# Chunk ends ahead of outputs in the S5 scan, and a bias table turned by TensorE

## What is computed

```python
def s5_mixer(u, ...):                     # 64 groups of 16 channels, 64 complex states each
    bu = einsum(u, bb)                    # inputs of the states
    s = associative_scan(a, bu)           # s[t] = a * s[t-1] + bu[t], over 512 steps
    y = einsum(s.re, c_re) - einsum(s.im, c_im) + d_skip * u
    y = gelu(y)
    return y * sigmoid(y @ w_glu + b_glu)
s5_branch = (s5_mixer(u) * silu(z)) @ w_out          # u, z = split(h @ w_in)

def sliding_window_attention(q, k, v, sinks, rel_bias):   # 16 heads, windows of 128
    s = q @ k.T * HEAD_DIM ** -0.5
    dist = qi + WINDOW - kj               # bias depends on the distance alone
    s = where(valid, s + rel_bias[t5_bucket(dist)], -1e30)
    p = softmax([s, sink]);  o = p @ v
```

## Time and profile before

| | |
|---|---|
| median of 3 runs | 3879.19 us (3876.99 to 3879.67) |
| the profiled execution: its own time | 3886.67 us |
| its span, first to last instruction | 3884.5 us |
| mean granted clock of TensorE | 0.951 of full |
| busy: TensorE, weight load | 92%, 71% |
| busy: VectorE, ScalarE, GpSimd | 58%, 28%, 37% |
| chain that ended last: TensorE, VectorE, issue, GpSimd | 71%, 15%, 7%, 3% |
| S5 scan, first flip to last y | 2565.5 to 2771.5 us |
| GLU product, output product | 2771.5 to 2839.3, 2839.3 to 2892.8 us |

### The profile page before, as it was taken

How to read it: one execution, slowest core, us unless ns; L and a number is a source line. 1 busy time by engine, 2 the same in 40 slices (tenths; PEclk the granted TensorE clock), 3 DMA queues, 4 the chain that set the end, 5 groups by cost and what they waited for, 6 DMA issues and landing times.

```text
span 3884.5 us, 44649 instructions
## 1 busy us (share of the span) xinstructions
PE 3576.9 (92%) x15779; PEld 2775.4 (71%) x15779; DVE 2239.8 (58%) x3073; ACT 1104.7 (28%) x1787; POOL 1424.2 (37%) x696
## 2 busy tenths in 40 slices
PE   6999999899998999999989999878879888999898
PEld 5888766678886888776678887667656565766676
DVE  5443487764434443378685433678564568476763
ACT  1222233322223222233332222311223442333332
POOL 3444553344443444453344444320122113311342
PEclk9999999999999999999899999986689889999999
DMA  3333321223333332332133323331262112211221
GB/s 100 95 88 96 96 71 41 68 86 94 89 95 88 94 95 88 99 88 54 28 93 96 96 87 104 75 91 48 73 114 60 33 38 64 57 36 44 78 87 55
DMA packets 622119, 299.40 MB, mean 77 GB/s; under 512 B 96925, under 2 KB 616590, under 8 KB 621982
## 3 DMA queue, kind: packets, MB, share of 16 engines
q1 hardware_dynamic: 618494, 287.50, 26.7%
q0 software_dynamic: 2592, 7.87, 1.2%
q10 hardware_dynamic: 896, 2.23, 0.2%
HBM read 287.58 MB, written 9.96 MB: 77 GB/s over the span
## 4 chain that ended last, share of the span: by engine, by line
PE 71%; DVE 15%; issue 7%; POOL 3%; ACT 3%; DMA 1%; DVEq 0%; SPq 0%; ACTq 0%; POOLq 0%
PE ps L319 21%; PE ps L328 21%; PE ps L320 21%; POOL WL L257 2%; PE ps L1002 2%; PE ps L2235 2%; POOL YP L1590 1%; PE ps L2233 1%; DMA RAW<-a_w_out 1%; DVE Y L1557 1%; PE ps L970 1%; DVE SS L421 1%; PE ps L991 1%; PE ps L489 1%; PE ps L1074 1%
## 5 line engine op out<-in xcount | busy, mean ns | idle before, releaser
L257 POOL TENSOR_TENSOR WL<-RAW,WH 128x1024 fp32r<-128x1024 f32 (+4 forms) x606 | 1314.7, 2171 | 2331.6 <-ACT WH L279 2331.4
L319 PE MATMUL ps<-UH,WH 128*128 128x512 f32 x3056 | 1246.7, 408 | 100.9 <-DVE UL L737 39.2
L320 PE MATMUL ps<-UL,WH 128*128 128x512 f32 x3056 | 1217.2, 398 | 0.0
L279 ACT ACTIVATE WH<-RAW 128x1024 fp32r<-128x1024 f32 (+4 forms) x605 | 570.9, 944 | 1333.1 <-PE ps L328 1288.1
L328 PE MATMUL ps<-UH,WL 128*128 128x512 f32 x3056 | 779.9, 397 | 11.0 <-POOL WL L257 11.0
L319 PEld LDWEIGHTS ps<-UH,WH 128*128 128x128 f32 x3056 | 589.5, 193 | 271.8 <-issue 56.7
L320 PEld LDWEIGHTS ps<-UL,WH 128*128 128x128 f32 x3056 | 589.3, 193 | 130.1 <-issue 7.6
L328 PEld LDWEIGHTS ps<-UH,WL 128*128 128x128 f32 x3056 | 576.4, 190 | 145.4 <-POOL WL L257 13.5
L1463 DVE TENSOR_TENSOR T<-ps,R 128x512 f32<-128x512 f32 x88 | 60.9, 691 | 392.7 <-PE ps L328 392.7
L319 PE MATMUL ps<-HH,WH 128*128 128x512 f32 x704 | 279.2, 397 | 0.0
L320 PE MATMUL ps<-HL,WH 128*128 128x512 f32 x704 | 276.9, 393 | 0.0
(11 more groups left out here) (432 smaller groups left out, 3972.0 us busy)
## 6 DMA issues: line engine op xcount, KB each, us to landing
RAW<-w_ff_in SPq DMA_DIRECT2D x176, 512.0 KB, 3.8
RAW<-w_in SPq DMA_DIRECT2D x72, 512.0 KB, 3.9
RAW<-w_ff_out SPq DMA_DIRECT2D x64, 384.0 KB, 3.2
RAW<-w_ff_out SPq DMA_DIRECT2D x64, 320.0 KB, 3.1
RAW<-d_w_in SPq DMA_DIRECT2D x24, 512.0 KB, 3.8
RAW<-b_w_in SPq DMA_DIRECT2D x17, 512.0 KB, 3.8
RAW<-w_out SPq DMA_DIRECT2D x16, 512.0 KB, 3.7
RAW<-w_ple_gate SPq DMA_DIRECT2D x16, 512.0 KB, 3.7
```

Of the source, the lines that this page charges most:

```text
L257: e.tensor_tensor(m.WL[:, s, 0:k, :], m.RAW[:, r, 0:k, :], m.WH[:, s, 0:k, :].bitcast(F32), ALU.subtract).then_inc(m.low_ready.sem, 1)
L279: e.activation(m.WH[:, s, 0:k, :], m.RAW[:, r, 0:k, :], ACT.Copy).then_inc(m.high_ready.sem, 1)
L319: e.matmul(out, m.WH[:, s, c, 0:t.cols], H[:, k0 + c, :], start=(x == 0 and c == 0), stop=False)
L320: e.matmul(out, m.WH[:, s, c, 0:t.cols], L[:, k0 + c, :], start=False, stop=False)
```

## The change

It has two parts.

1. In Chunks.tensor the block of ends(k) stands ahead of the block of y(k-1), with all its waits. Nothing else of S5 is touched.
2. The bias table. BROW goes to DRAM once (skew, 16 x 384, 24 KB) from SP's queue. SP reads BIAS from it with a partition step of one element, so that partition q has the shift P-1-q: the table upside down. A new step Turnover multiplies it by a reversed identity (FLIP, a new constant, loaded with the others) in eight matmuls of 128x512 (two heads each) and copies each product back into BIAS on ScalarE. Turnover runs inside Renorm, behind the root. The loads go out at unit 2, the one-hot matmul and its VectorE steps behind tile 2, the write at unit 6, the read at unit 7; GpSimd's two DMAs and the step Unskew go. BiasReady and the value flip wait for the copies.

```diff
@@ -702,6 +702,8 @@
         m.next_root = None
+        self.beside = m.beside_root
+        m.beside_root = None
         self.x0 = m.x_new.reserve(DC)
@@ -714,10 +716,14 @@
         self.root.tensor(e)
+        if self.beside is not None:
+            self.beside.tensor(e)
...
         self.root.scalar(e)
+        if self.beside is not None:
+            self.beside.scalar(e)
         if self.next_gain is None:
@@ -2221,6 +2228,18 @@
                             yield
+                        if k < DC:
+                            e.wait_ge(inputs_ready.sem, k + 1)
+                            e.wait_ge(u2_in[k], 16 * TC)
+                            if k > 0:
+                                e.wait_ge(states_ready.sem, k)
+                            for n in range(2):
+                                for t in range(4):
+                                    for g in range(2):
+                                        ins = e.matmul(m.ps[half(g), 7, (4 * n + t) * NC:(4 * n + t + 1) * NC], L1[:, n, t, half(g)],
+                                                       U2[:, 4 * k + t, g, :], start=True, stop=True)
+                            ins.then_inc(ends_made.sem, 1)
+                            yield
                         if k >= 1:
@@ -2235,18 +2254,6 @@
                             ins.then_inc(y_made.sem, 1)
-                            yield
-                        if k < DC:
-                            e.wait_ge(inputs_ready.sem, k + 1)
-                            e.wait_ge(u2_in[k], 16 * TC)
-                            if k > 0:
-                                e.wait_ge(states_ready.sem, k)
-                            for n in range(2):
-                                for t in range(4):
-                                    for g in range(2):
-                                        ins = e.matmul(m.ps[half(g), 7, (4 * n + t) * NC:(4 * n + t + 1) * NC], L1[:, n, t, half(g)],
-                                                       U2[:, 4 * k + t, g, :], start=True, stop=True)
-                            ins.then_inc(ends_made.sem, 1)
                             yield
@@ -2420,21 +2427,22 @@
                         cu.go("sync", e)
+                    if j == 2:
+                        rel_load.issue(e)
                     if j == 6:
-                        rel_load.issue(e)
+                        e.wait_ge(m.flip_free.sem, rel.b + 1)
+                        e.dma_start(skew, BROW[:]).then_inc(skewed, 16)
+                    if j == 7:
+                        e.wait_ge(skewed, 16)
+                        e.dma_start(BIAS[:], bass.AP(skew.tensor, 0, [[1, P], [3 * P, SWA_HEADS], [1, 2 * P]])).then_inc(skewed, 16)
                 def tensor_tail(self, e, i, n):
-                    if n == 6:
+                    if n == 2:
                         rel.tensor(e)
...
                 def vector_tail(self, e, i, n):
-                    if n == 6:
+                    if n == 2:
                         rel.vector(e)
-
-                def gpsimd_tail(self, e, i, j):
-                    if j == 7:
-                        e.wait_ge(m.flip_free.sem, rel.b + 1)
-                        e.dma_start(skew.rearrange("h q x -> h q x"), BROW[:].unsqueeze(1).to_broadcast([SWA_HEADS, P, 3 * P])).then_inc(skewed, 16)
             add(RestOfChunks(cu))
@@ -2455,27 +2463,40 @@
                 return f
-            rel_load = Load([(RELB[0:32, :], a["rel_bias_2"], swa_in), (RELB[32:33, :], a["c_masked"], swa_in), (HOT[:], a["c_hot"], swa_in),
+            rel_load = Load([(RELB[0:32, :], a["rel_bias_2"], swa_in), (RELB[32:33, :], a["c_masked"], swa_in), (HOT[:], a["c_hot"], swa_in), (FLIP[:], a["c_flip"], swa_in),
                              (SINK[:], a["b_sinks_2"][0].partition_broadcast(P), swa_in)])
...
             def rel_pe(e, bank):
-                e.wait_ge(swa_in, 64)
+                e.wait_ge(swa_in, 80)
                 return e.matmul(bank[0:SWA_HEADS, 0:3 * P], RELB[:], HOT[:], start=True, stop=True)
...
                 e.wait_ge(*v.last)
-                e.wait_ge(swa_in, 64)
+                e.wait_ge(swa_in, 80)
                 e.tensor_scalar(SINK[:], SINK[:], 8.0, None, ALU.mult).then_inc(*v.next())
-            class Unskew(Step):
-                def gpsimd(self, e):
-                    e.wait_ge(skewed, 16)
-                    src = bass.AP(skew.tensor, P - 1, [[3 * P - 1, P], [P * 3 * P, SWA_HEADS], [1, 2 * P]])
-                    e.dma_start(BIAS[:], src).then_inc(skewed, 16)
+            class Turnover(Step):
+
+                b0, o0 = bias_turned.reserve(SWA_HEADS // 2), bias_out.reserve(SWA_HEADS // 2)
+                flips = m.flips.total
+
+                def tensor(self, e):
+                    e.wait_ge(skewed, 32)
+                    e.wait_ge(m.flip_free.sem, self.flips)
+                    for g in range(SWA_HEADS // 2):
+                        if g > 1:
+                            e.wait_ge(bias_out.sem, self.o0 + g - 1)
+                        e.matmul(m.ps[:, 4 + g % 2, :], FLIP[:], BIAS[:, 2 * g:2 * g + 2, :], start=True, stop=True).then_inc(bias_turned.sem, 1)
+
+                def scalar(self, e):
+                    for g in range(SWA_HEADS // 2):
+                        e.wait_ge(bias_turned.sem, self.b0 + g + 1)
+                        e.activation(BIAS[:, 2 * g:2 * g + 2, :], m.ps[:, 4 + g % 2, :].rearrange("p (h x) -> p h x", h=2),
+                                     ACT.Copy).then_inc(bias_out.sem, 1)
             wg = chunks(a["a_w_glu_2"][0])
@@ -2483,7 +2504,7 @@
             out_gemm(chunks(a["a_w_out_2"][0]), UF, (M2H, M2L), gg.s0)
-            add(Unskew())
+            m.beside_root = Turnover()
@@ -2512,7 +2533,8 @@
                 return ins
-            fl = Flips(m, [(turn_values, lambda g, e, bank: e.tensor_copy(VB[:], bank.rearrange("p (t x) -> p t x", x=P)).then_inc(*g.frees()))])
+            fl = Flips(m, [(turn_values, lambda g, e, bank: e.tensor_copy(VB[:], bank.rearrange("p (t x) -> p t x", x=P)).then_inc(*g.frees()))],
+                       needs=[(bias_out.sem, bias_out.total)])
             fl.t0 = m.tiles + 1
@@ -2530,7 +2552,7 @@
                 def vector(self, e):
-                    e.wait_ge(skewed, 32)
+                    e.wait_ge(bias_out.sem, bias_out.total)
             add(BiasReady())
@@ -2908,7 +2930,8 @@
         k_dram = nc.dram_tensor("k_dram", [DC, P, P], F32, kind="Internal").ap()
-        skew = nc.dram_tensor("skew", [SWA_HEADS, P, 3 * P], F32, kind="Internal").ap()
+        skew = nc.dram_tensor("skew", [SWA_HEADS, 3 * P], F32, kind="Internal").ap()
+        bias_turned, bias_out = [Signal(ctx.enter_context(nc.semaphore(n))) for n in ("bias_turned", "bias_out")]
...
```

More of the change, by code:

```diff
@@ L1319, in build @@
             BIAS = sb("BIAS", [P, SWA_HEADS, 2 * P], F32, ph)
+            FLIP = sb("FLIP", [P, P], F32, ph)
         with ExitStack() as ph:
@@ L1450, in build @@
                   needs=[(const_in, 16 * 4)], splits=DC, squares=DC))
-        m.next_root = None
+        m.next_root = m.beside_root = None
         def ffn(l, w_in, w_out, next_gain):
@@ L2976, in constants @@
             "c_tri": (np.arange(P)[:, None] <= np.arange(P)[None, :]).astype(np.float32), "c_selg": selg,
-            "c_ident": np.eye(P, dtype=np.float32),
+            "c_ident": np.eye(P, dtype=np.float32), "c_flip": np.eye(P, dtype=np.float32)[::-1].copy(),
             "c_mask": np.where(np.arange(P)[None] > np.arange(P)[:, None], np.float32(MASKED), np.float32(0))}
```

## The result

The changed kernel takes 3897.48 us (median of 7 runs, 3894.09 to 3904.32), the one before 3879.67 in the same comparison (7 runs): ratio 1.0042, interval 1.0032 to 1.0052, so 16.3 us slower (12.4 to 20.2). The forecast was 3891 with a range of 3878 to 3901. The profiled execution of the changed kernel took 3898.65 us, its span is 3896.7 and its granted clock 0.950. Against the profiled execution of before (3886.67, span 3884.5) this is +12.2 in the span.

A forecast was written before the change was run, and what follows sets the result against it. TensorE, busy 92% of the span, was taken as the bound. S5 +20 and bias table -8.0 made +12 on the profiled 3886.67 us, 3898.7; less the profile's 7.5 above the median, 3891, range 3878 to 3901.

The forecast's parts named there:

- The loop behind the GEMM: S5 groups 4 to 7: y starts 13.0 us after the CA_ fill in three intervals, +6.0 us in sum.
- The last step gains nothing: S5, y(7): still waits for MT loads behind y(6)'s stores, 9.3 us from store to y(7); no gain.
- Rival B: S5's last step: y(7) starts on its states, some 2.5 us sooner, moved ends hidden; total 3869; chance 0.05.
- The woven intervals: S5 groups 0 to 3, inside the GEMM: y slips behind moved tile halves, ends and copies; +14 us taken.
- Rival A: S5 tiles 4 to 7: moved halves are absorbed, part 1 costs 6 to 8, total 3877 to 3879; chance 0.16.
- the difference carries over: Whole kernel: the profiled execution's 7.5 us above the median holds after the change too, so 3898.7 becomes 3891.
- VectorE beside GpSimd: Last GLU tiles: L2453 gives back 4.1 us spent beside the write, L2455 takes 2.2 more in two tiles; sum 0.
- Rival C: Output product: the 2048 KB read takes 23 us and holds output weights 4 to 8 us, 3895 to 3899; chance 0.08.
- a sign of being wrong: Output product: a_w_out weight units landing after more than 10 us would show the forecast wrong.
- Rival D: Behind the root: the turnover runs at the low clock, +9 instead of +2.5, total 3898; chance 0.06.

The follow-up runs named there:

- e3_rest: The kernel before with ends(k) ahead of y(k-1) only for k = 5, 6 and 7, behind the GEMM: 3889.47 us, ratio 1.0016.
- e7_l1first: The changed kernel with ScalarE's L1 copy made before it waits for the states: 3892.92 us, ratio 1.0028 to the kernel before.
- e11_swap: The changed kernel with the MT(k) loads ahead of the stores of y(k-1) in SP's queue: 3891.58 us, ratio 1.0027 to the kernel before.
- e9_busy: The kernel before with eight added TensorE products behind the root whose results nobody reads: 3883.19 us, ratio 0.9998.
- e2_bias: The kernel before with the new bias table alone, S5 in the old order: 3872.49 us, ratio 0.9976.
- e10_two: e2_bias with two of the turnover's eight groups ahead of the root's product: 3871.4 us, ratio 0.9968 to the kernel before.
- e12_best: e10_two with ends(7) ahead of y(6) in the last group alone and MT loads ahead of y stores: 3865.64 us, ratio 0.9957 to the kernel before.
- e5_glu: e2_bias with the turnover's groups behind GLU tiles 5, 6 and 7 instead of behind the root: 3876.7 us, ratio 0.9986 to the kernel before.
- e6_split: The kernel before with the 3072 KB BROW write halved by heads, second half behind the output product: 3886.71 us, ratio 1.0018.
- e8_rows: The kernel before with the 3072 KB BROW write halved by rows, second half behind the output product: 3874.13 us, ratio 0.9981.

## Why the prediction was right, and by how much it was off

**Sign and mechanism: right.** The change is slower, through part 1, and part 2 gives back about half of it.

**The loop behind the GEMM: right to the decimal.** Forecast 13.0 us from fill to y in three intervals; measured 12.9, 13.0 and 12.9 (the middle one is 2717.81 to 2730.83). Forecast +6.0; measured +6.0 between the two profiles, 6.0 or 6.7 in e3_rest by what it is held against. e7_l1first shows the copy in that chain to be real.

**The last step gains nothing: right, and for the reason given.** From store to y(7) 9.4 us, forecast 9.3. e11_swap took the loads away from behind the stores and freed 9.1 us. Rival B (3869) named the same gain and fell by just this; it put it at 2.5 us, which is what the old order leaves between states and y(7); with ends(7) ahead the states are ready as soon as y(6) is read, and it is 9.1.

**The woven intervals: right in kind, short at two.** From fill to y: y(1) 17.1 forecast, 16.95 measured; y(2) 17.6 and 19.7; y(3) 17.6 and 18.5. The step that fell short is the clock. Before y(2), TensorE stands 2.35 us for the L1 copy; the ends take 1.97 us where I had 1.15, and the high half runs from 2648.45 to 2654.24, 5.8 us where I had 4.5. Before y(3) the high half runs from 2673.61 to 2678.90, 5.3 us where I had 4.5. Rival A, that these halves are absorbed, fell with the same rows: the wait before ends(3) is 2.35 us, and TensorE stands 3.01 us for a bank before the high half that y(3) is behind. (Ends(2) waits 0.57 us only, and there the forecast was over by 0.15.)

That the three intervals still came out near the sum (+13.2 forecast, +11.9 between the profiles) is luck. From fill to y they grew by 16.0 us. But the outputs' own matmuls, which the forecast left as they were, took 12.39, 9.95 and 10.45 us before and 9.99, 9.24 and 9.48 after, 4.1 less; in before y(1) ran at a mean granted clock of 0.54.

**The step that failed: "the difference carries over".** The forecast for the profiled execution was 3898.7 and it took 3898.65. That is partly luck, since +2.9 us of it lie before S5, where nothing was changed, and -4.7 in the attention stage, which I had at zero; the part inside the woven intervals is named above. But then I took off the 7.5 us by which the profile of before lay above its median; the profile of the change lies 1.2 us above its own (3898.65 against 3897.48). That the difference didn't carry over is shown. Where it lay is argued from the table: the old order of S5 has a long pattern, 25.0 and 25.4 us for intervals 0-1 and 2-3 (before, e3_rest and, with 25.2 and 25.5, e9_busy, which has 24.2 instead of 21.6 between them too), and a short one, 22.8 to 23.0 and 22.8 (e2_bias, e10_two, e12_best and also e5_glu, e6_split, e8_rows). TensorE in the first y of e2_bias and of before:

```profile
2621.38 1.11 PE L2242 MATMUL ps<-HS,CA_ 64*128 64x64 f32 x4
```

```profile
2616.96 1.08 PE L2235 MATMUL ps<-HS,CA_ 64*128 64x64 f32 x4
```

These are the first of the y(1) matmuls at the low clock (1.1 us for four, 0.66 before them): the fifth group of four in e2_bias, already the second in before, 1.3 us after y(1) began instead of 4.2. The profile that I worked from had the long pattern, 4.7 us more than the short one. The reorder's intervals replace either pattern, so part 1 costs +19.5 against that profile and +23.9 against e2_bias's, and by medians +26 (21 to 31). A sum made against a profile above its median needs the place of the excess; where it lies in the intervals that the edit rewrites, it doesn't carry over. If the median execution of before has the short pattern, these 4.7 us are the larger part of the 6.5 by which 3891 was short. No run shows that it has: the profiles with the long pattern lie 7.0, 7.1 and 0.2 us above their medians (before, e3_rest, e9_busy), those with the short one from 6.9 below (e6_split) to 5.9 above (e2_bias), so the pattern isn't all of it.

**Part 2: the sum was right, its parts less so.** Forecast -8.0; e2_bias -9 (-14 to -4). From the last gelu to the first UH the profiles give -6.0, and I can name -10.5 for the stall (as forecast), +1.0 for BROW and SINK in GLU tile 3 (I had 0: a tile takes 7.47 us there instead of 6.48), +0.6 for the output product's second tile at the low clock (6.22 us against 5.57), +0.8 for the root's product (1.91 against 1.12), +2.2 for the turnover (I had 2.5). That is -5.9. The other part of the gain lies in the attention stage and wasn't foreseen.

**VectorE beside GpSimd: right in the sum, wrong in one cause.** L2461 takes 1.06 and L2463 2.85 us in the last tiles, which cancels the 5.15 and 0.69 of the earlier trace rows, as the sum had it. But the prediction put the 5.15 us of L2453, from 2832.21 on, down to the write. GpSimd's row of before shows two weight steps there, late behind its wait for BROW:

```profile
2831.89 4.65 POOL L257 TENSOR_TENSOR WL<-RAW,WH 128x1024 fp32r<-128x1024 f32 x2
```

In e6_split and e8_rows, with half the write, L2453 takes 5.23 and 4.88 us beside the same 4.65. It is the same meeting of the two engines, beside two steps instead of one. The 3.67 us of e8_rows shows it at another place.

**Rival C** fell by the read's landing after 10.6 us: it moves some 193 KB per us, where the write that the rival took its pace from moved 90. Its price didn't follow from its own numbers either, as 23 and 3.8 us against a cover of 26 are under 1 us late, not 4 to 8. In kind it was nearer than it looks: beside the read three weight units landed after 11.7, 11.7 and 10.4 us, past the 10 us that the prediction named as a sign of being wrong, and only the cover made that cost nothing. So the sign was badly chosen. **Rival D** was half right: the root's product ran at the low clock (1.91 us), but the turnover behind it at a mean granted clock of 0.89 (2910.4 to 2918.5 us), 8.27 us for sixteen passes. And the idle stretch that D blamed doesn't decide it: behind the same 2.35 us the root's product took 1.12 in before and 1.13 in e7_l1first, where the turnover took 7.32.

## What to carry to other kernels

Before an operation is moved ahead of another in an engine's order, list what each waits for: if the one moved ahead waits for more, the other inherits that wait in every round, and here the inherited chain (copy, ends) gave the loss behind the GEMM to a tenth of a us. Check the last round apart, and ask what stands behind the step in the DMA queue: the reorder paid only there, some 3 us by an estimate, and only once eight small loads no longer stood behind eight stores. When the profile lies above the median, ask in which stretch, before the difference is carried over: here the profile of before lay 7.5 us above, that of the change 1.2.

## What the runs showed of the hardware

The time of a broadcast write to DRAM hangs on how its outermost dimension is cut: 1536 KB took 34.7 us with 8 outermost and 17.9 us with 16, at a DMA share of 0.49 and 0.94. Weight units of 512 KB landed after 32.0 us beside the 3072 KB write, after 10.4 to 11.7 beside a 2048 KB read and after 3.7 alone. A VectorE step with two inputs in SBUF took 3.67 us beside a GpSimd weight step of 2.36 (0.69 without), and one of 1.06 us took 5.15 beside two weight steps, 4.65 together. One root product of TensorE took from 1.12 to 2.08 us behind the same idle stretch of 2.35 us in eleven profiles; with two products in that stretch (e10_two, e12_best) it took 1.12. The same S5 code ran in more than one pattern: intervals 0-1 to 2-3 took 67.4 us in e2_bias, 72.0 in before and 74.8 in e9_busy. In before and e2_bias TensorE's clock falls at different places of y(1). What decides between the patterns stays open.
